# Attention probabilities turned in blocks of 32 by VectorE and placed by ScalarE, instead of turned on TensorE

## What is computed

```
sc = q @ k.T * 128**-0.5 + bias          # layer 0: relative bias; layer 1: differences of cumulative log gates
sc = where(allowed, sc, NEG_INF)         # queries of block 0 see keys of block 0, block 1 sees both
p  = softmax(sc)
o  = p @ v
x  = x + (o * silu(g)) @ w_out           # over all heads of the layer
```

## Time and profile before

| | |
|---|---|
| time, median of 3 runs | 2439.96 us (2438.97 to 2440.54) |
| profiled execution: time | 2439.27 us |
| profiled execution: span from first to last instruction | 2437.5 us |
| PE busy | 2408.9 us, 99% |
| DVE busy | 1759.7 us, 72% |
| ACT busy | 1223.9 us, 50% |
| POOL busy | 307.3 us, 13% |
| mean granted TensorE clock | 0.999 |

### The profile page before, as it was taken

How to read it: one execution, slowest core, us unless ns; L and a number is a source line. 1 busy time by engine, 2 the same in 40 slices (tenths; PEclk the granted TensorE clock), 3 DMA queues, 4 the chain that set the end, 5 groups by cost and what they waited for, 6 DMA issues and landing times.

```text
span 2437.5 us, 40472 instructions
## 1 busy us (share of the span) xinstructions
PE 2408.9 (99%) x16588; PEld 2151.4 (88%) x16588; DVE 1759.7 (72%) x2629; ACT 1223.9 (50%) x1811; POOL 307.3 (13%) x401
## 2 busy tenths in 40 slices
PE   7999999999999999999999999999999999999998
PEld 7999999888888888888888888888888888888887
DVE  8998797896767676757666669767576757676766
ACT  6555433675544454445444556554454445444545
POOL 1222114432100000000000001200011001000101
PEclk9999999999999999999999999999999999999999
DMA  8666773386666666675766666767676767767764
GB/s 221 176 160 176 199 184 91 104 223 193 189 187 181 193 182 188 189 188 174 188 196 182 193 169 192 195 180 190 195 187 191 185 190 182 195 187 196 186 176 121
DMA packets 758344, 443.31 MB, mean 182 GB/s; under 512 B 28784, under 2 KB 721136, under 8 KB 758160
## 3 DMA queue, kind: packets, MB, share of 16 engines
q1 hardware_dynamic: 752880, 430.16, 63.9%
q0 software_dynamic: 5280, 10.56, 2.9%
HBM read 437.35 MB, written 3.31 MB: 181 GB/s over the span
## 4 chain that ended last, share of the span: by engine, by line
PE 81%; DVE 3%; issue 1%; ACT 0%; DVEq 0%; ACTq 0%
PE bank L295 40%; PE bank L299 20%; PE bank L325 5%; PE bank L326 5%; PE bank L329 5%; PE bank L1886 1%; PE bank L1901 1%; PE bank L1891 1%; PE bank L1885 1%; PE bank L1902 1%; DVE splitb L260 0%; PE bank L275 0%; PE bank L277 0%; PE bank L276 0%; DVE splita L260 0%
## 5 line engine op out<-in xcount | busy, mean ns | idle before, releaser
L295 PE MATMUL bank<-xx,splitb 128*128 128x512 f32 x3328 | 1154.8, 394 | 1.5 <-DVE mix L2183 0.8
L260 DVE TENSOR_TENSOR splitb<-rawb,splitb 128x1024 fp32r<-128x1024 f32 x672 | 837.3, 1255 | 379.4 <-ACT splitb L254 372.0
L254 ACT ACTIVATE splitb<-rawb 128x1024 fp32r<-128x1024 f32 x672 | 702.1, 1055 | 477.9 <-PE bank L299 325.4
L299 PE MATMUL bank<-xx,splitb 128*128 128x256 f32 x3328 | 920.6, 277 | 0.0
L295 PEld LDWEIGHTS bank<-xx,splitb 128*128 128x128 f32 x3328 | 625.0, 188 | 132.5 <-DVE mix L2183 1.1
L299 PEld LDWEIGHTS bank<-xx,splitb 128*128 128x128 f32 x3328 | 625.0, 188 | 2.4
L295 PE MATMUL bank<-oo,splitb 128*128 128x512 f32 x1008 | 343.3, 389 | 0.0
L275 PE MATMUL bank<-xhl,splita 128*128 128x258 f32 (+1 forms) x1040 | 297.7, 286 | 11.8 <-DVE splita L260 10.6
L277 PE MATMUL bank<-xhl,splita 128*128 128x258 f32 (+1 forms) x1040 | 292.9, 282 | 0.0
L276 PE MATMUL bank<-xhl,splita 128*128 128x258 f32 (+1 forms) x1040 | 292.6, 281 | 0.0
L299 PE MATMUL bank<-oo,splitb 128*128 128x256 f32 x1008 | 278.3, 276 | 0.0
(11 more groups left out here) (298 smaller groups left out, 2255.3 us busy)
## 6 DMA issues: line engine op xcount, KB each, us to landing
rawb<-in_a_w_in_dram SPq DMA_DIRECT2D x256, 512.0 KB, 4.8
rawa<-in_w_in_dram SPq DMA_DIRECT2D x130, 512.0 KB, 5.3
rawb<-in_kv_w_dram SPq DMA_DIRECT2D x128, 512.0 KB, 4.8
rawb<-in_b_w_in_dram SPq DMA_DIRECT2D x128, 512.0 KB, 5.4
rawb<-in_a_w_out_dram SPq DMA_DIRECT2D x64, 512.0 KB, 5.2
rawb<-in_b_w_out_dram SPq DMA_DIRECT2D x64, 512.0 KB, 5.2
rawb<-in_w_out_dram SPq DMA_DIRECT2D x32, 512.0 KB, 5.2
table<-in_rel_dram POOLq DMA_DIRECT2D x32, 128.0 KB, 4.8
```

The lines of the kernel that those rows point to most:

```text
L254: nc.scalar.activation(self.parts(at, h)[0], self.raw_half(at, h), ACT.Copy).then_inc(hi_ready, 1)
L260: nc.vector.tensor_tensor(lo, self.raw_half(at, h), hi.bitcast(F32), ALU.subtract).then_inc(lo_ready, 1)
L295: nc.tensor.matmul(out, hi[:, w], both(k).rearrange("p a t -> p (a t)"), start=start and k == 0, stop=False)
L299: last = nc.tensor.matmul(out[:, 0:SEQ], lo[:, w], both(k)[:, 0], start=False, stop=stop and k == 7)
```

## The change

`turn_probs` and `take_probs` go. In their place DVE, right after the shares, turns the tile `pr` of 128 x 384 with one instruction into the tile `sc`, whose scores are no longer needed. This instruction turns each block of 32 x 32 where it stands. The blocks of 32 are then in the wrong place: for each of the three 128 x 128 blocks, block (row c, column b) must go to (row b, column c). ACT does this in `move_probs`: sixteen copies a head, one for each pair of quadrants (b, c), each of 32 partitions x 3 x 32 elements, in two batches (h = 0 and 1) of eight.

In ACT's queue the batches of head `j - 1` stand in step `j`: the first behind the q unit's `move_cross` and the second behind the k unit's. In steps 1 and 2 both stand behind the k unit's. Head 7 has no step 8 with q and k: both its batches stand at the end of step 7, behind `take_gated(5)`. There are two tiles `pT`, used in turn, and `sc` is now also the source of the copies. So DVE waits for the copies of the head before (`pt_taken`) ahead of its next `maxima`, and at two later places that write to `sc`; ACT waits, ahead of a head's first batch, for the weighing that last read its `pT` tile.

```diff
-    sc, pr, pT = (sbuf(ph, n, [P, W3]) for n in ("sc", "pr", "pT"))
+    sc, pr = (sbuf(ph, n, [P, W3]) for n in ("sc", "pr"))
...
+    pT = [sbuf(ph, f"pT{b}", [P, W3]) for b in range(2)]
+    NQ, QB = 4, 32
...
-                    def turn_probs(j):
-                        pe.wait_ge(p_ready, head_no(layer, g, j) * 2 + 2)
-                        for m in range(3):
-                            last = nc.tensor.transpose(PT[:, P * m:P * m + P], pr[:, P * m:P * m + P], ident[:])
-                        last.then_inc(tr_ready, 1)
-
                     def weigh(j):
                         pe.wait_ge(v_taken, block_no(layer, g, j // VB) * 2 + 2)
-                        pe.wait_ge(pt_taken, head_no(layer, g, j) + 1)
+                        pe.wait_ge(pt_taken, 2 * head_no(layer, g, j) + 2)
...
                             if j >= 2:
                                 weigh(j - 2)
-                            if 1 <= j <= GH:
-                                turn_probs(j - 1)
                             if j < GH:
                                 scores(j)
...
-                    def take_probs(j):
-                        act.wait_ge(tr_ready, head_no(layer, g, j) + 1)
-                        a(pT[:], PT[:, 0:W3], ACT.Copy).then_inc(pt_taken, 1)
+                    def move_probs(j, h):
+
+                        n = head_no(layer, g, j)
+                        if h == 0:
+                            act.wait_ge(tr_ready, n + 1)
+                            wait(act, o_sum, n - 1)
+                        for b in (2 * h, 2 * h + 1):
+                            keys = slice(QB * b, QB * b + QB)
+                            for c in range(NQ):
+                                rows = slice(QB * c, QB * c + QB)
+                                ins = a(pT[n % 2][keys].rearrange("k (m q) -> k m q", m=3)[:, :, rows],
+                                        sc[rows].rearrange("q (m k) -> q m k", m=3)[:, :, keys], ACT.Copy)
+                        ins.then_inc(pt_taken, 1)
...
                             split(q)
-                            if j == 2:
-                                take_probs(0)
                             if 1 <= j <= LAG:
                                 exps(j - 1)
                             move_cross(q)
+                            if j > LAG:
+                                move_probs(j - 1, 0)
                             split(k)
                             move_cross(k)
+                            if 1 <= j <= LAG:
+                                move_probs(j - 1, 0)
+                            if j >= 1:
+                                move_probs(j - 1, 1)
                         if j >= LAG:
                             at = place(layer, g, "g", j - LAG)
                             ahead(split_hi, at, 0)
-                            if j <= GH:
-                                take_probs(j - 1)
                             ahead(split_hi, at, 1)
                             if j < GH:
                                 exps(j)
                             gate(at)
                             take_gated(j - LAG)
+                            if j == GH - 1:
+                                move_probs(j, 0)
+                                move_probs(j, 1)
...
                         dve.wait_ge(sc_sum, n + 1)
+                        wait(dve, pt_taken, 2 * n)
...
                             ts(pr[:, parts[m]], pr[:, parts[m]], stat[:, 4 + m:5 + m], None, ALU.mult).then_inc(p_ready, 1)
+                        dve.wait_ge(p_ready, head_no(layer, g, j) * 2 + 2)
+                        v_.transpose(sc[:], pr[:]).then_inc(tr_ready, 1)
```

More of the change, by code:

```diff
@@ L1541, in _build @@
     f_ones = sbuf(ph, "f_ones", [AH, SEQ])
-    SC, PT, OT, FZ = psum[2:6]
+    SC, _, OT, FZ = psum[2:6]
     OUTS = [OT, FZ]
@@ L1900, in weigh @@
                         w = slice(j % VB * P, (j % VB + 1) * P)
-                        nc.tensor.matmul(OUTS[j % 2][:, 0:SEQ], vtm[:, 0, w], pT[:, 0:SEQ], start=True, stop=False)
-                        nc.tensor.matmul(OUTS[j % 2][:, P:SEQ], vtm[:, 1, w], pT[:, SEQ:W3], start=False,
+                        probs = pT[j % 2]
+                        nc.tensor.matmul(OUTS[j % 2][:, 0:SEQ], vtm[:, 0, w], probs[:, 0:SEQ], start=True, stop=False)
+                        nc.tensor.matmul(OUTS[j % 2][:, P:SEQ], vtm[:, 1, w], probs[:, SEQ:W3], start=False,
                                          stop=True).then_inc(o_sum, 1)
@@ L2220, in second_norms @@
                 dve.wait_ge(f_part, 1)
+                dve.wait_ge(pt_taken, 2 * AH)
                 tt(f_parts, FP, inv, ALU.mult).then_inc(f_scaled, 1)
@@ L2354, in _ @@
                 dve.wait_ge(norm_root, 4 + q)
+                dve.wait_ge(pt_taken, 2 * 2 * AH)
                 v_.reciprocal(invc[:, q:q + 1], invc[:, q:q + 1]).then_inc(norm_inv, 1)
```

## The result

The changed kernel takes 2513.28 us (median of 4 runs, 2511.86 to 2517.83), the kernel before beside it 2440.07 (2438.97 to 2440.54). The ratio is 1.030, with a 95% interval of 1.029 to 1.032: 73 us slower. I had forecast 2442 and a range up to 2462, so the forecast is wrong.

The account below looks back on a forecast made before the run. PE, 99% busy, was taken to bound the kernel. From 2439.27 us: -21.1 for the turns, +21.2 and +1.6 for stalls at group ends and starts, +0.5 in layer 1, 2441.5, given as 2442; 8-in-10 range 2428 to 2462.

Parts of the forecast that it names:

- What goes: On PE, the three turns of each head go, 0.33 us a head, 21.1 us over 64 heads, all gained.
- The turn on DVE: On DVE after the shares, one 128x384 turn a head, assumed 0.55 us, range 0.41 to 2.6.
- What comes on ACT: Sixteen copies a head on ACT, 266 ns each but overlapping: 2.5 us more a head, nearly all beside PE.
- p: Time from one ACT block copy to the next in a run: 0.18 us taken, upper end 0.28.
- the copies cost their full length: Rival: ACT copies do not overlap, p 0.26 to 0.28, 2468 to 2474 us; all cases slower than 2445 together 0.37.
- 3.2 us for each 0.01 of p: Sensitivity of total time to the copy step: 40 copies a group count, 8 + 16 + 16.
- The end of a group: At the projection's start, head 7's copies delay DVE's clearing of g7; PE stalls 2.65 us, eight times, 21.2 us.
- The start of a group: Head 0's sixteen copies delay the clearing of k; PE stalls about 0.2 us at the scores, 1.6 us in all.
- In between: Heads 3 to 7: 1.5 us in hand against two batches of 8, so no stall up to p about 0.27.

Follow-up runs that it names:

- the run with the assumed price: Changed kernel with sixteen copies a head of 64 partitions instead of 32, blocks not put in place: 2455.24 us, ratio 1.006 against the kernel before.

## Why the prediction was wrong

**What goes.** Right: 0.33 us a head, 0.30 to 0.33 measured wherever nothing stalls. The turn on DVE too: 0.579 us, 0.55 assumed.

**The step that failed: "What comes on ACT. ... I take p = 0.18."** The duration was right within 14 ns (266 forecast, 280 measured); the overlap was not. I took it from four neighbours that all begin at partition 0 and applied it to copies that change quadrants every time. p is 0.29. I had named this case ("the copies cost their full length", 0.26 to 0.28) and laid its cause to strided runs across quadrants. The runs do not matter; the quadrants do, not within a copy but from one copy to the next. And I gave the case too little weight, and left it out of the range. Its price was too low as well: by my 3.2 us for each 0.01 of p, 0.29 gives 2442 + 35 = 2477, while the overlap measured 58 us between two runs. What else was missing stands below.

**The end of a group.** The working holds within 0.3 us. With p = 0.29, 24 copies add 24 x 0.11 = 2.64 us to the 2.65: 5.29 us. Measured are 4.98 + 0.33 = 5.31 where the clock does not fall. That they agree to 0.02 is partly luck: in the run with 64 partitions, where sixteen copies take 1218.18 - 1215.25 = 2.93 us (0.18 each, the step assumed), it is 2.64 + 0.33 = 2.97 against 2.65. PE's idle time there, 2.66, is what I had worked out; of the 0.3 more, 0.2 are the price of a stall above its idle time.

**The start of a group.** Too low. 0.2 + 16 x 0.11 = 1.96 against 1.93 + 0.33 + 0.35 = 2.61 at the second distance (PE idle for 1.52 + 0.61 us, and twice 0.2 on top), and another 1.04 + 0.33 = 1.37 at the third, which I had not stepped through: head 2's two batches come on a queue that is still late. In the run with 64 partitions it is 0.17 + 0.33 + 0.35 = 0.85 instead of 0.2.

**In between.** "Nothing stalls there up to about 0.27" agrees with the runs: -0.31 at 0.18, and at 0.29 losses of 0.13 and 0.48 us by turns. Where between the two they begin was not measured.

**What I had not put in.** The price of a stall above its idle time (12 us in all), and the clock (13 us). Neither is in the trace before, where PE never waits in these layers. With the start of a group they explain most of the 13 us by which the run with the assumed price missed 2442: per group 1.01 was measured where I had (-21.1 + 21.2 + 1.6)/8 = 0.21, 6.4 us in eight groups, and at the ends of three groups the clock fell (1.5, about 3 and about 1.5 us); the rest lies at the first group's start.

What stays open: why the clock fell at six stalls of 3.03 us and not at two like them, why a change of partitions takes the overlap away, and why PE's tiles at the start of a group are slower in the kernel before. None of them was tried further. Nor were the copies tried on VectorE, where sixteen took 3.66 us by themselves.

## What to carry to other kernels

An overlap is a matter of two neighbours, not of one instruction; take it only from neighbours that stand to each other as yours will (here: that begin on other partitions each time), and where there are none, take the full duration as the likeliest value. When a job is moved to an engine with room on average, look at the ends of the loop, where steps are short and batches pile up: here the two ends of each group carried most of the loss, and moving the job only in the middle, to the idlest engine, turned +3.0% into -0.5%. Count a stall of TensorE as its idle time and 0.2 us more, and one of 3 us as perhaps costing 1.4 to 2.8 us more through the clock.

## What the runs showed of the hardware

- ScalarE, float32 copies of 96 elements from SBUF to SBUF: a step of 0.174 us with 128 or 64 partitions when all begin on the same one, 0.291 with 32 when each begins on another quadrant than the one before. With 64 partitions the overlap of 0.09 to 0.10 us is lost in just the places where the half changes.
- VectorE: 579 ns for the turn of 128 x 384 in blocks of 32; 16 copies of 32 x 96 in 3.66 us, a step of 0.23.
- GpSimd: 16 copies of 32 x 96 in 4.78 us by themselves, 8.2 to 9.4 us when each waits for the one before and the other engines are busy.
- A DMA of 12 KB issued from ScalarE's queue holds it for 0.65 us.
- TensorE, around 3 us without a matmul: a granted clock of 0.50, the 1.2 GHz level, in six cases of eight, and 1.4 to 2.8 us lost by it. A stall costs 0.2 us above its idle time.
